# Three layers on one core: z before values, attention in pairs of units, gates weighed on GpSimd, small products on column tiles

## The reference, cut to what matters

```python
a, b = proj[..., P + 4*G : P + 4*G + 8]        # 8 columns of w_in: gates of the delta rule
# sparse attention: three branches, each with a gate for each head
q, kc, vc, ks, vs, kw, vw, gates, z = split(h @ w_in)
gates = sigmoid(gates)                         # 48 columns: 3 branches x 16 heads
k_cmp, v_cmp = silu(blk @ w1) @ w2             # compressed keys and values, 31 of them
o_c = masked_softmax(q @ k_cmp.T - slope*dist) @ v_cmp
o_s = masked_softmax(q @ ks.T - slope*dist) @ vs
o_w = masked_softmax(q @ kw.T - slope*dist) @ vw
o = (g0*o_c + g1*o_s + g2*o_w) * silu(z)
# state-space part: a chunked scan; y = lag matrix @ u + C powers @ state
```

## Time and profile before

| | us |
|---|---|
| median of 3 runs (1314.68 to 1316.49) | 1314.89 |
| the profiled execution | 1314.87 |
| its span, first to last instruction | 1313.1 |
| PE busy / PEld busy | 1271.4 / 1000.9 |
| DVE / ACT / POOL busy | 748.1 / 415.8 / 806.7 |

### The profile page before, as it was taken

One profiled execution on the slowest core, in us unless ns is written; L12 is line 12 of the kernel. 1 busy time (PEld: TensorE's weight loads), 2 busy tenths in 40 slices (PEclk: granted clock), 3 DMA queues, 4 the chain that ended last, 5 costly groups with the idle time before them and its releaser, 6 DMA issues.

```text
span 1313.1 us, 21036 instructions
## 1 busy us (share of the span) xinstructions
PE 1271.4 (97%) x7698; PEld 1000.9 (76%) x7698; DVE 748.1 (57%) x1101; ACT 415.8 (32%) x851; POOL 806.7 (61%) x742
## 2 busy tenths in 40 slices
PE   7999999999999999999999999899999999999996
PEld 5778997878877888888788798455557787878884
DVE  5978665589498111695446235278874559722223
ACT  4175745353201133212200021477772201331111
POOL 7766622878799677898678617212214774457772
PEclk9999999999999999999999999899999999999998
DMA  5222100443326433345493203000005369523331
GB/s 206 88 74 72 50 3 16 114 128 102 96 74 209 159 97 96 114 143 155 131 344 116 75 25 98 31 1 1 1 1 208 114 153 271 203 73 97 96 96 72
DMA packets 86627, 137.94 MB, mean 105 GB/s; under 512 B 16528, under 2 KB 34448, under 8 KB 85520
## 3 DMA queue, kind: packets, MB, share of 16 engines
q1 hardware_dynamic: 48384, 88.10, 22.0%
q10 hardware_dynamic: 38160, 48.71, 11.9%
HBM read 119.02 MB, written 20.91 MB: 107 GB/s over the span
## 4 chain that ended last, share of the span: by engine, by line
PE 82%; DVE 8%; POOL 4%; ACT 2%; issue 1%; DMA 1%; ACTq 1%; DVEq 0%; POOLq 0%
PE ps L403 20%; PE ps L405 20%; PE ps L404 20%; PE ps L839 3%; PE ps L819 3%; PE ps L863 3%; POOL wl L1485 2%; PE ps L573 2%; POOL wh L1483 2%; PE ps L723 1%; PE ps L768 1%; PE ps L927 1%; PE ps L563 1%; DVE bigA L1655 1%; DVE bigA L2093 1%
## 5 line engine op out<-in xcount | busy, mean ns | idle before, releaser
L1485 POOL TENSOR_TENSOR wl<-raw,wh 128x512 fp32r<-128x512 f32 x336 | 495.7, 1475 | 26.9
L1483 POOL CAST wh<-raw 128x512 fp32r<-128x512 f32 x336 | 261.9, 780 | 299.4 <-PE ps L405 257.3
L403 PE MATMUL ps<-uH,wh 128*128 128x512 f32 x664 | 261.6, 394 | 1.3 <-DVE uL L1578 1.3
L405 PE MATMUL ps<-uH,wl 128*128 128x512 f32 x664 | 258.5, 389 | 0.0
L404 PE MATMUL ps<-uL,wh 128*128 128x512 f32 x664 | 258.4, 389 | 0.0
L403 PEld LDWEIGHTS ps<-uH,wh 128*128 128x128 f32 x664 | 124.7, 188 | 29.0 <-DVE uL L1578 1.7
L404 PEld LDWEIGHTS ps<-uL,wh 128*128 128x128 f32 x664 | 124.7, 188 | 26.8 <-issue 1.4
L405 PEld LDWEIGHTS ps<-uH,wl 128*128 128x128 f32 x664 | 124.6, 188 | 26.1
L403 PE MATMUL ps<-ffH,wh 128*128 128x512 f32 x256 | 101.0, 394 | 2.7 <-POOL wl L1485 2.7
L404 PE MATMUL ps<-ffL,wh 128*128 128x512 f32 x256 | 99.8, 390 | 0.0
L405 PE MATMUL ps<-ffH,wl 128*128 128x512 f32 x256 | 99.7, 389 | 0.0
(11 more groups left out here) (404 smaller groups left out, 2334.5 us busy)
## 6 DMA issues: line engine op xcount, KB each, us to landing
raw<-wstream SPq DMA_DIRECT2D x336, 256.0 KB, 2.6
b_powers_scratch<-bigB ACTq DMA_DIRECT2D x4, 1024.0 KB, 4.8
c_powers_scratch<-bigB ACTq DMA_DIRECT2D x8, 512.0 KB, 4.2
lags_scratch<-lag_rows_scratch ACTq DMA_DIRECT2D x8, 512.0 KB, 8.8
bigB<-b_powers_scratch ACTq DMA_DIRECT2D x4, 1024.0 KB, 9.6
bigB<-lags_scratch ACTq DMA_DIRECT2D x4, 1024.0 KB, 6.5
bigB<-c_powers_scratch ACTq DMA_DIRECT2D x4, 1024.0 KB, 9.9
hT<-x ACTq DMA_DIRECT2D x4, 512.0 KB, 7.5
```

Source lines behind the costliest of these rows:

```text
L403: pe.matmul(out, lh, rh, start=first, stop=False)
L405: return pe.matmul(out, ll, rh, start=False, stop=last)
L1483: pool.tensor_copy(wh[:, j, :], raw[:, j, :]).then_inc(half_lead, 1)
L1485: pool.tensor_tensor(wl[:, j, :], raw[:, j, :], wh[:, j, :].bitcast(f32), ALU.subtract).then_inc(half_split, 1)
```

## The change

**Small projections.** `side_by_side` multiplies unsplit fp32 weights, with the norm's weights multiplied in by GpSimd (`scale_small`), with the residual hT: eight matmuls, k by k on four column strips of 32 (a and b) or two of 64 (gates). The strips are added where the result is transposed, by a matmul against a stacked identity.

**State-space parts.** `lag_kernels` is called twice, after tiles 2 and 5, for two column strips each, so that four different tiles (two row halves, two column strips) follow one another. In `chunk_outputs` the halves are crossed for the last four pairs, so that four different tiles of 64 x 64 follow one another too (the stored order of the pairs is changed to match).

**Order.** zed comes before val, with the compressed part among its tiles; its probabilities are padded from 31 to 32 columns, so that 16 transposes of 128 x 128 take the place of 64, and the compressed values use four row groups by two column halves. They are put aside on ScalarE. The scores of the first three pairs are made between half slots of val, in banks 4 to 7. ScalarE and VectorE share the eviction of val.

**Attention.** Units come in pairs, (0, 3) and (2, 1); LAG is 3 pairs. GpSimd multiplies the exponentials by reciprocal sum and gate before they are turned (`weigh`), so that both branches of t add up in one PSUM bank: `spread`, L1550 and most of VectorE's finishing are gone. GpSimd splits the result (`split_branches`). `values` follows the last `turn` of its group with only one `scores` between.

```diff
-SLOTS = dict(inp=20, out=8, up0=16, down0=16, up1=16, down1=16, nsa=16, val=4, zed=8, nout=8, sin=16, glu=16, sout=8)
-TILES = dict(inp=20, out=8, up0=16, down0=8, up1=16, down1=8, nsa=16, val=4, zed=8, nout=8, sin=16, glu=16, sout=8)
+SLOTS = dict(inp=20, out=8, up0=16, down0=16, up1=16, down1=16, nsa=16, zed=8, val=4, nout=8, sin=16, glu=16, sout=8)
...
+            def side_by_side(bank, strips, w):
+                c = 128 // strips
+                for k in range(KT):
+                    strip = k % strips
+                    i = pe.matmul(ps[strip * c:(strip + 1) * c, bank, :], w[:, k * c:(k + 1) * c], hT[:, k, :],
+                                  start=k < strips, stop=k >= KT - strips)
+                return i
...
+            pe.wait_ge(wab_scaled, 1)
+            side_by_side(5, 4, w_ab).then_inc(ab_ready, 1)
...
-            def lag_kernel(c):
-                pe.wait_ge(ca_done, c + 1)
+            def lag_kernels(c):
+                pe.wait_ge(ca_done, c + 2)
                 if c == 0:
                     pe.wait_ge(bt_ev, 16)
                 for n in range(8):
-                    pair = c * 8 + n
                     for ri in range(2):
-                        for half in range(2):
-                            P = slice(64 * half, 64 * half + 64)
-                            i = pe.matmul(ps[32 * c:32 * c + 32, 4 + n // 4 * 2 + half, n % 4 * 128:n % 4 * 128 + 128],
...
-                i.then_inc(k_mm, 1)
+                        for at in (c, c + 1):
+                            pair = at * 8 + n
+                            for rows in range(2):
+                                P = slice(64 * rows, 64 * rows + 64)
+                                half = rows if n < 4 else 1 - rows
+                                i = pe.matmul(ps[32 * at:32 * at + 32, 4 + n // 4 * 2 + half, n % 4 * 128:n % 4 * 128 + 128],
...
+                i.then_inc(k_mm, 2)
...
-            down(1, {t: lambda c=c: lag_kernel(c) for c, t in enumerate((1, 2, 3, 5))})
+            down(1, {t: lambda c=c: lag_kernels(c) for c, t in ((0, 2), (2, 5))})
...
+            side_by_side(6, 2, w_gate).then_inc(g_mm, 1)
...
+            def scores(n):
+                t, b, g, qts = unit_pair(n)
+                if n == 0:
+                    pe.wait_ge(cs_ev, TT + KT)
+                if n == LAG:
+                    pe.wait_ge(tile_evicted, TILE0["val"] + TT)
+                for i, qt in enumerate(qts):
+                    before = 2 * n + i - 1
+                    if before > 0:
+                        pe.wait_ge(at_s, before)
+                    for half in range(2):
...
+                for i, qt in enumerate(qts):
+                    pe.wait_ge(at_w, 2 * n + i + 1)
+                    if qt == 2:
+                        pe.wait_ge(at_dve, g + 1)
+                    elif qt == 1:
+                        pe.wait_ge(at_act, 3 * g + 1)
+                    elif g:
+                        pe.wait_ge(at_act, 3 * g - (1 if qt == 3 else 0))
...
             def values(g):
                 t, b = g // 2, g % 2
-                pe.wait_ge(at_long, 2 * g + 2)
-                pe.wait_ge(at_short, 2 * g + 2)
-                if g:
-                    pe.wait_ge(at_g, 2 * g)
-                else:
-                    pe.wait_ge(cs_p, TT + KT)
+                pe.wait_ge(at_dve, g + 1)
+                pe.wait_ge(at_act, 3 * g + 3)
+                if t and not b:
+                    pe.wait_ge(at_g, t)
                 for kt in range(TT):
                     for half in range(2):
                         h = t // 4 * 2 + half
                         i = pe.matmul(ps[64 * half:64 * half + 64, 7, kt * 128:512], vtok[:, kt, b * 256 + h * DH:b * 256 + (h + 1) * DH],
-                                      probT[g % 2][:, half, kt, kt * 128:512], start=kt == 0, stop=kt == TT - 1)
+                                      probT[g % 2][:, half, kt, kt * 128:512], start=b == kt == 0, stop=b == 1 and kt == TT - 1)
                 i.then_inc(at_v, 1)
...
+            cmp_hidden()
+            zed_tile(0)
+            gate_turn()
+            cmp_products()
+            zed_tile(1)
+            cmp_scores()
+            for n in range(2, 6):
+                zed_tile(n)
+            cmp_turn(0)
+            zed_tile(6)
+            cmp_turn(1)
+            zed_tile(7)
+            cmp_turn(2)
+            cmp_turn(3)
+            val_slot(0)
+            cmp_values(0)
+            val_slot(1)
+            cmp_values(1)
+            val_slot(2)
+            val_slot(3)
+            scores(0)
+            val_slot(4)
+            val_slot(5)
+            scores(1)
+            val_slot(6)
+            val_slot(7)
+            scores(2)
+            turn(0)
+            scores(3)
+            for n in range(LAG + 1, PAIRS + LAG + 1):
+                if n < PAIRS:
                     scores(n)
-                if n < 2:
-                    for t in range(4 * n, 4 * n + 4):
-                        cmp_values(t)
-                if LAG <= n < len(UNITS) + LAG:
+                if n >= LAG + 2 and n % 2:
+                    values((n - LAG - 2) // 2)
+                if n < PAIRS + LAG:
                     turn(n - LAG)
...
-                        for half in range(2):
-                            P = slice(64 * half, 64 * half + 64)
-                            o = ps[P, 6 + p // 4, p % 4 * 128:p % 4 * 128 + 128]
+                        for rows in range(2):
+                            half = half_of(p, rows)
+                            P = slice(64 * rows, 64 * rows + 64)
+                            o = ps[64 * half:64 * half + 64, 6 + p // 4, p % 4 * 128:p % 4 * 128 + 128]
...
+            for n in range(LAG, PAIRS + LAG + 1):
+                m = n - LAG - 1
+                if m >= 0:
+                    if m % 2 == 0:
+                        evict_turned(m // 2, 0, 2 * m)
+                    else:
+                        evict_turned(m // 2, 2, 2 * m)
+                        evict_turned(m // 2, 1, 2 * m + 1)
+                if n < PAIRS:
+                    exps(n)
...
+            def weigh(n):
+                t, b, g, qts = unit_pair(n)
+                pool.wait_ge(cs_sub, TT + n + 1)
+                for i, qt in enumerate(qts):
+                    for half in range(2):
+                        h = half * 8 + t
+                        p = prob_place(n, qt, half)
+                        m = pool.tensor_scalar(p, p, rsum[:, n % NBUF, i, half:half + 1], gate[:, qt, 1 + b, h:h + 1], ALU.mult, ALU.mult)
+                    m.then_inc(at_w, 1)
+            def split_branches(t):
+                pool.wait_ge(x_full, NHG + t + 1)
+                pool.tensor_copy(uH[:, t, :], xs[:, t % 2, :]).then_inc(x_lead, 1)
+                pool.wait_ge(x_lead, NHG + t + 1)
+                pool.tensor_tensor(uL[:, t, :], xs[:, t % 2, :], uH[:, t, :].bitcast(f32), ALU.subtract).then_inc(at_o, 1)
...
+            split_weights(2 * SLOT0["zed"] + 8, 2 * SLOT0["nout"])
+            for n in range(PAIRS):
+                weigh(n)
+                if n == LAG:
+                    split_weights(2 * SLOT0["nout"], 2 * SLOT0["nout"] + RING)
+                if n % 4 == 3 and n // 4 + 2 < KT:
+                    slopes(n // 4 + 2)
+                if n % 4 == 1 and n >= 9:
+                    split_branches(n // 4 - 2)
+            split_branches(KT - 2)
+            split_branches(KT - 1)
...
+            def branches(t):
+                dve.wait_ge(at_v, 2 * t + 2)
+                if t >= 2:
+                    dve.wait_ge(at_o, t - 1)
+                dve.tensor_tensor(xs[:, t % 2, :], ps[:, 7, :], cmpT[t], ALU.add).then_inc(at_g, 1)
+                dve.wait_ge(at_g, t + 1)
+                dve.tensor_tensor(xs[:, t % 2, :], xs[:, t % 2, :], zsT[:, t, :], ALU.mult).then_inc(x_full, 1)
+            for n in range(PAIRS + LAG + 1):
+                m = n - LAG - 1
+                if n == LAG:
+                    for tt in range(2, TT):
+                        dve.wait_ge(half_used, 2 * SLOT0["val"] + KT)
+                        dve.tensor_scalar(vtok[:, tt, :], ps[:, tt, :], rcol[:, tt:tt + 1], None, ALU.mult).then_inc(tile_evicted, 1)
+                if m >= 0 and m % 2 == 0:
+                    evict_longest(m // 2)
+                if n < PAIRS:
                     shift(n)
+                if 1 <= n <= PAIRS:
+                    invert(n - 1)
+                if n == 8:
+                    dve.wait_ge(zs_gated, 8)
+                    dve.wait_ge(cs_ev, TT + KT)
+                if n >= 8 and n % 4 == 0:
+                    branches(n // 4 - 2)
+            branches(KT - 1)
...
```

548 lines of the change are left out of this document (250 added, 298 removed).

## The result

The changed kernel takes 1296.14 us (median of 4 runs, 1294.58 to 1301.28), the kernel before 1315.69 beside it; the ratio is 0.986 (95% interval 0.984 to 0.988). The forecast was 1296 us.

| stretch | forecast | by the traces | from, before and after |
|---|---|---|---|
| start to the lag matrices (a and b product) | 0 | 0.0 | the half slot at 499.66 is at 499.66 |
| lag matrices (down1) | -6.2 | -4.2 | nsa's first matmul 644.01, 639.85 |
| gate product to nout | -8.0 | -10.6 | 728.77 to 994.07, 724.58 to 979.25 |
| third layer, nout to glu | -4.5 | -3.2 | 994.07 to 1168.31, 979.25 to 1150.33 |

What follows compares the result with a forecast made beforehand. TensorE was taken as the bound almost everywhere, with a three-engine loop setting the changed attention's pace. From 1314.9 us, 8 (gate product to nout), 6.2 (lag matrices) and 4.5 (chunk outputs) came off: 1296 us, range 1287 to 1304.

Steps and rivals of the forecast that it cites:

- The loop through three engines: Attention: TensorE, VectorE and ScalarE wait in a circle, 9.5 us a group, TensorE standing some 1.6 us before `values`.
- The attention as a whole: Gate product to nout: parts sum to 257.3 us against 265.3, a gain of 8.
- The fill is hidden by val, which is the real gain here: Attention start: scores of pairs 0 and 1, 2.9 us, go between val slots, so val hides the fill.
- The lag matrices: Lag calls in down1: 128 records in about 4 us against 7.2; 6.2 us less in the forecast sum.
- VectorE stands idle 10.68 us: Powers of C: third and fourth come some 10 us later, but VectorE's idle time lets later tiles be evicted in time.
- The chunk outputs: Third layer: 16 records in 0.55 us against 1.02; three calls give 5.6, taken as 4.5, bounds 0 and 5.6.
- The first call's gain is lost: Chunk outputs: of 1.9 us a call, the first call's goes, as L907 behind it waits for a DMA.
- The a and b product: Small projection: TensorE only waits longer for VectorE at L518; taken as 0, bounds gain 1 and loss 1.
- Rival 1: Small-tile parts: four tiles run no faster than two, so the last two terms go, 1307 us; 15%.
- column strips on the same rows gain nothing: Small tiles: by the skill's rule, no gain beyond the two overlapping row halves; the trace disagrees for two column tiles.
- The clock rival: Attention: clock falls as TensorE stands still more; six groups low would be 39 us more, 1335 us; 3%.

Runs made afterwards that it cites:

- the early-input run: Changed kernel with VectorE evicting input tile 5 between the first chunk's two scans and ScalarE regrouping chunk 2 earlier; 1289.64 us, ratio 0.981.
- the strip-by-strip kernel: Changed kernel with the small projections' matmuls of one column strip in a row (two each for a and b, four for gates); 1297.9 us, ratio 0.987.
- the kernel with the turn first: Changed kernel with only TensorE's order altered, `values` behind the turn of the next pair (0, 3); 1292.74 us, ratio 0.983.

## Why the forecast was right, and where it was not

- *The loop through three engines:* right in place, engine and size (9.37 against 9.5), and shown from both sides: ScalarE's order takes it away, TensorE's does not.
- *The attention as a whole, -8, was -10.6.* Every piece came a little short of its price: gate product 3.6 (3.7), the rest of the compressed part 23.9 (25.7, no stall for the table load is seen), 16 transposes 1.5 (2.1), compressed values 2.1 (2.6), thirteen groups 121.9 (123.5); only the end was dearer, 18.5 (17), since its last `values` ran at a low clock (0.59 on the mean of 976 to 979.2). The start, from the end of val to the first `values`, took 12.7 (13.1). What paid was the stretch ahead of the first `values`, 21.4 us shorter. The groups themselves lost: from the first `values` to nout 129.6 us before, 140.4 after.
- *"The fill is hidden by val, which is the real gain here"* was wrong: hiding the scores is worth about 2 us. The gain is in the transposes (11.7 to 1.5) and in what ran at a granted clock of 0.50 before, 17 us, and now does not. Which of the new orders keeps the clock up there was not tried.
- *The lag matrices, -6.2, were -4.2.* The step that failed is "VectorE stands idle 10.68 us": I asked only whether VectorE keeps up. The rate was better than forecast (28 ns, not 32, 7.2 us gained), but TensorE then stood 2.7 us for GpSimd's split of the weights, and 0.3 more is lost about these waits. Here is GpSimd beside VectorE's powers of C, in the changed kernel:

```profile
556.40 1.74 POOL L1557 CAST wh<-raw 128x512 fp32r<-128x512 f32 x1
558.21 2.26 POOL L1559 TENSOR_TENSOR wl<-raw,wh 128x512 fp32r<-128x512 f32 x1
...
566.71 0.61 POOL L1557 CAST wh<-raw 128x512 fp32r<-128x512 f32 x1
567.40 1.28 POOL L1559 TENSOR_TENSOR wl<-raw,wh 128x512 fp32r<-128x512 f32 x1
```

```profile
555.33 2.33 DVE L1995 TENSOR_TENSOR bigB<-bigB 128x1152 f32<-128x1152 f32 x1
557.70 1.65 DVE L1996 TENSOR_TENSOR bigB<-bigB 128x1152 f32<-128x1152 f32 x1
559.38 2.32 DVE L1997 TENSOR_TENSOR bigB<-bigB 128x1152 f32<-128x1152 f32 x1
```

While VectorE works on two operands from SBUF, a half slot costs GpSimd 4.0 us, more than TensorE's 12 x 0.227 = 2.72; alone it costs 1.9. GpSimd's times are the same before (1.74 at 556.39, 2.26 at 558.21). There a lag call of 3.6 us at 557 let it catch up; the first call is now at 570, and TensorE pays. The Trainium skill, "SBUF — State Buffer", section "SBUF: two separate sides", says that GpSimd and a VectorE instruction with two SBUF inputs share ports under a lock that one holds for a whole instruction. The trace agrees: GpSimd's cast starts inside one instruction of VectorE (it ends at 557.66) and its subtraction inside the next, each ends 0.5 to 1.1 us after that one, and both are back to 0.61 and 1.28 at 566.71, when VectorE has stood idle from 565.6 on. That the first call's place is what makes TensorE pay is read from the two traces; no run moves the calls.
- *The chunk outputs, -4.5, were -3.2.* 37 ns a record (35 forecast), 6.8 us off TensorE's list. "The first call's gain is lost" held, and the pause costs 1.5 us more: L969 takes 3.5 us, not 2.0, with a granted clock of 0.72 on the mean of 1086 to 1092. The two edits around it give all of that back.
- *The a and b product, 0:* 0.0 in the trace. TensorE's waits for VectorE there grew from 0.9 to 3.5 us (2.5 at L533 and 1.1 at L539), where the forecast had about 4.
- *Rival 1 (four tiles no faster than two)* is refuted by the changed kernel (28 and 37 ns) and by the two runs that go back to two tiles (52 and 73). With it falls, for these tiles, what the forecast drew from the rule of the Trainium skill ("TensorE: Matmul & The Clock Gate", section "The mechanism"), that column strips on the same rows gain nothing: they brought 52 ns down to 28. The same section also lets a weight load go ahead into a background buffer, and no run here tells by which way it does. The Trainium skill's page "TensorEngine Tiling (Array Packing)", section "Key Properties", says that different tiles load weights and multiply in parallel, and the runs agree in the time of the two together.
- *The clock rival (3%)* was thought of too coarsely. The granted clock did not fall for whole groups but for one `values`, in some executions. The profiled execution of the early-input run shows it; two rows of its timeline, and one window:

```profile
868.65 4.07 PE L905 MATMUL ps<-bigB,bigA 128*64 128x512 f32 x16 [1.81 <-ACT bigB L1394]
...
879.69 2.37 PE L905 MATMUL ps<-bigB,bigA 128*64 128x512 f32 x16 [1.76 <-ACT bigB L1394]
```

```profile
870.00:872.00 2.00, 2.00 (x9) 0.96 (x7) 0.00 (x0) 0.68 (x4) 2.00 (x5) 0.50 0.00 0
```

Behind a wait of 1.81 us the clock is at 0.50, the level of 1.2 GHz, `values` takes 4.0 us instead of 2.3, and the group 11.05 instead of 9.37. Behind the next one, 1.76 us, it is not. In this execution five groups of the first ten did so, every second one, 8.4 us; in that of the changed kernel only the last `values`. This fits the spread of the changed kernel's runs (1294.6 to 1306.6 us, the longer at the lower mean clock) and the 4 us (1272.3 to 1275.9) without the wait, but it isn't shown: five runs of the strip-by-strip kernel, with the same waits of 1.8 us, lie within 2.1 us, four of the kernel with the turn first within 3.7, and the kernel before spreads by 8 us (1312.7 to 1321.2) with at most 0.9 us of waiting in a group.

## What to carry to other kernels

When an engine waits, edit the list of the engine that it waits for: here the same two instructions, moved ahead of two exponentials whose result was not yet waited for, were worth 22 us between the profiled executions (26 between the medians), and moving the waiting instruction 2.7. Before crediting work taken off the bounding engine, add up the next engine's time in that very stretch, at the speed that it has beside its neighbour. And a short pause that comes back in each turn of a loop can cost more than its length, where the clock falls behind it (1.7 us more on a group here, in some executions): look at the spread of the runs, not only at the median.
